# Feed-forward input chunks as seven block products over half the tokens, with d_ff in two groups

## What is computed

```python
x = x + 0.5 * swiglu_ffn(rms_norm(x, ffn1_norm), ffn1_w_in, ffn1_w_out)
h = rms_norm(x, mix_norm)
q, k, v, xr, gate = split(h @ w_in_proj)        # differential attention | RG-LRU branch
x = x + concat([y_attn, y_rnn]) @ w_out_proj
x = x + 0.5 * swiglu_ffn(rms_norm(x, ffn2_norm), ffn2_w_in, ffn2_w_out)

def swiglu_ffn(h, w_in, w_out):
    g, u = split(h @ w_in, 2)
    return (silu(g) * u) @ w_out
```

## Time and profile before

| | before |
|---|---|
| median of 3 runs | 938.46 us (938.35 to 939.8) |
| time of the profiled execution | 938.35 us |
| its span, first to last instruction | 936.5 us |
| TensorE busy | 922.3 us, 98% |
| VectorE busy | 482.4 us, 52% |
| ScalarE busy | 331.1 us, 35% |
| DMA engines, mean | 27% |

### The profile page before, as it was taken

The page is one execution under the profiler, slowest core; times in us unless marked ns, Lnnn a source line. Parts: engine busy times, 40 slices in busy tenths (PEclk is TensorE's granted clock), DMA queues, the critical chain, the costliest instruction groups (busy, mean ns, idle before and its releaser), DMA issues.

```text
span 936.5 us, 11101 instructions
## 1 busy us (share of the span) xinstructions
PE 922.3 (98%) x4154; PEld 754.2 (81%) x4154; DVE 482.4 (52%) x712; ACT 331.1 (35%) x526; POOL 3.1 (0%) x25
## 2 busy tenths in 40 slices
PE   8999999999999999999997999999999999999998
PEld 7888888888888888777885678888888888888887
DVE  6754444444444346665879776645444444422221
ACT  7422222332223233356647654332222233211220
POOL 0000000000000000000000000000000000000000
PEclk9999999999999999999999999999999999999999
DMA  7222222222222224222221022322233222132241
GB/s 272 97 90 95 113 106 90 90 90 76 90 95 92 92 95 154 97 83 90 91 90 45 1 91 70 111 90 90 90 105 119 90 90 76 63 122 92 92 140 42
DMA packets 16295, 89.13 MB, mean 95 GB/s; under 512 B 2064, under 2 KB 2192, under 8 KB 8976
## 3 DMA queue, kind: packets, MB, share of 16 engines
q1 hardware_dynamic: 16128, 88.32, 27.1%
q0 software_dynamic: 144, 0.52, 0.2%
HBM read 86.74 MB, written 2.10 MB: 95 GB/s over the span
## 4 chain that ended last, share of the span: by engine, by line
PE 95%; DVE 2%; ACT 1%; DMA 1%; issue 1%; SPq 0%; ACTq 0%
PE bank L975 31%; PE bank L977 30%; PE bank L976 30%; PE bank L1172 1%; PE bank L1115 1%; PE bank L1149 1%; DMA raw<-w_in_dram 1%; PE bank L1162 0%; PE bank L1089 0%; DVE h_lo L599 0%; DVE small L896 0%; ACT w_hi L341 0%; PE bank L990 0%; ACT sq L518 0%; DVE yr_lo L803 0%
## 5 line engine op out<-in xcount | busy, mean ns | idle before, releaser
L975 PE MATMUL bank<-h_hi,w_hi 128*128 128x512 f32 x768 | 301.4, 392 | 0.9 <-DVE w_lo L587 0.8
L977 PE MATMUL bank<-h_hi,w_lo 128*128 128x512 f32 x768 | 298.9, 389 | 0.0
L976 PE MATMUL bank<-h_lo,w_hi 128*128 128x512 f32 x768 | 298.9, 389 | 0.0
L587 DVE TENSOR_TENSOR w_lo<-raw,w_hi 128x1024 fp32r<-128x1024 f32 (+1 forms) x178 | 188.7, 1101 | 79.5 <-ACT w_hi L341 73.9
L341 ACT ACTIVATE w_hi<-raw 128x1024 fp32r<-128x1024 f32 (+1 forms) x178 | 160.9, 951 | 159.9 <-PE bank L977 159.9
L975 PEld LDWEIGHTS bank<-h_hi,w_hi 128*128 128x128 f32 x768 | 144.1, 188 | 32.9 <-DVE w_lo L587 1.2
L976 PEld LDWEIGHTS bank<-h_lo,w_hi 128*128 128x128 f32 x768 | 144.2, 188 | 30.9 <-issue 1.2
L977 PEld LDWEIGHTS bank<-h_hi,w_lo 128*128 128x128 f32 x768 | 144.2, 188 | 30.1
L975 PE MATMUL bank<-act_hi,w_hi 128*128 128x512 f32 x352 | 136.9, 389 | 0.0
L976 PE MATMUL bank<-act_lo,w_hi 128*128 128x512 f32 x352 | 136.9, 389 | 0.0
L977 PE MATMUL bank<-act_hi,w_lo 128*128 128x512 f32 x352 | 136.9, 389 | 0.0
(11 more groups left out here) (173 smaller groups left out, 656.7 us busy)
## 6 DMA issues: line engine op xcount, KB each, us to landing
raw<-w_in_dram SPq DMA_DIRECT2D x43, 1024.0 KB, 4.8
raw<-w_out_dram SPq DMA_DIRECT2D x32, 704.0 KB, 4.0
raw<-w_qkv_dram SPq DMA_DIRECT2D x6, 1024.0 KB, 4.8
raw<-w_rnn_dram SPq DMA_DIRECT2D x4, 1024.0 KB, 4.7
raw<-w_proj_dram SPq DMA_DIRECT2D x4, 1024.0 KB, 4.8
x<-xT_dram SPq DMA_DIRECT2D x8, 256.0 KB, 6.0
out_dram<-x SPq DMA_DIRECT2D x8, 256.0 KB, 5.0
raw<-w_in_dram SPq DMA_DIRECT2D x4, 256.0 KB, 6.0
```

What stands on the lines that cost most here:

```text
L587: dve.tensor_tensor(w_lo[:, part], raw[:, part], w_hi[:, part].bitcast(F32), ALU.subtract).then_inc(low_made, 1)
L975: pe.matmul(dst, s_hi, m_hi, start=first, stop=False)
L976: pe.matmul(dst, s_hi, m_lo, start=False, stop=False)
L977: return pe.matmul(dst, s_lo, m_hi, start=False, stop=last)
```

## The change

Of the 22 input chunks of each feed-forward, the first 4 (ffn1) or 2 (ffn2) stay as they were ("P", plain). The others ("W") compute gate and up for all 512 tokens by Strassen's scheme in its form by Winograd: the weights of a pair of k-tiles are a 2 x 2 of 128x128 blocks (k parity by gate or up), the two k-tiles of h another 2 x 2 of 128x256 blocks (k parity by earlier or later 256 tokens). In place of eight block products there are seven, `seven_products`, each over 4 pairs and three parts, 84 products of 256 columns. Ops 1, 4 and 6 take weight blocks as they are, ops 0, 2, 3 and 5 take sums of them; ops 0, 2, 3 and 6 take sums of blocks of h (T1 to T4). Ops 3 to 6 add onto what ops 0 to 2 left in three half banks, after it has been read.

- GpSimd makes T1 to T4 once for each feed-forward (`blocks_of_h`), ScalarE and VectorE their highs and lows (`t_highs`, `t_lows`).
- VectorE makes the four weight sums (`s123`, `s4`) and their lows (`s_lows`); ScalarE their highs (`s_highs`).
- The lows of the three plain blocks: ScalarE writes the negated highs (`minus_highs`), and an SBUF to SBUF transfer from GpSimd's queue adds the raw weights onto them (`a_lows`).
- ScalarE copies two partial results (`copies`); VectorE combines the seven into gate and up (`take_q6` to `up_later`).

d_ff is worked in groups of 10 and 12 tiles: 10 input chunks, 8 output chunks of 10 k-tiles, 12 input chunks, 8 output chunks of 12. Each output tile is therefore taken out of PSUM twice. Half rstd multiplies there, no longer in up. The programs of SP, ScalarE and VectorE are unrolled in the feed-forwards; TensorE keeps its loops. The sine and exponential of ScalarE stand under the first group's output chunks. The core of the diff (added lines; what is left out are counts, layout, and the same helpers without their slot argument):

```diff
+GROUP = (10, 12)
+FIRST_TILE = (0, GROUP[0])
+PLAIN = (4, 2)
...
+        t_hi = region("t_hi", [P, 2 * KT * SEQ], F32R, tile_at(36))
+        t_lo = region("t_lo", [P, 2 * KT * SEQ], F32R, tile_at(52))
...
+        B12, B11, B22, B21, T1, T2, T3, T4 = range(8)
+        MOVING = (T2, B11, T1, T3, B21, B22, T4)
+        def s_place(op, s):
+            at = {1: s * SLOT, 4: s * SLOT + BLOCK, 6: s * SLOT + 2 * BLOCK, 0: A_COLS, 5: SLOT + A_COLS, 2: 0, 3: BLOCK}[op]
+            return (ws_hi, ws_lo, at) if op in (2, 3) else (w_hi, w_lo, at)
+        def s_parts(op):
+            hi, lo, at = s_place(op, 0)
+            return hi[:, at:at + BLOCK], lo[:, at:at + BLOCK]
+        S_OPS = (0, 2, 3, 5)
...
+        def part_bank(c, n):
+            return bank[3 * (c % 2) + n][:, 0:HALF]
...
+        T_STEPS = (((), (0,), (1, 2), (3,)), ((0, 1), (2, 3)))
...
+            def consumed(c):
+                if kind(c) == "W":
+                    w = wino_of(c)
+                    sp.wait_ge(high_made, 2 * c + 2)
+                    sp.wait_ge(s13_made, 2 * w + 2)
+                    sp.wait_ge(s4_made, w + 1)
+                    sp.wait_ge(low_landed[c % 2], 16 * (w // 2 + 1))
+                else:
+                    sp.wait_ge(low_made, lows_through(c))
...
+            def blocks_of_h(f):
+                gain_col = (COL_G1, COL_G2)[f]
+                pool.wait_ge(h_low, 2 * KT * f + KT)
+                for p in range(KT // 2):
+                    buf = pairbuf[p % 2]
+                    b = lambda n: buf[:, n * HALF:(n + 1) * HALF]
+                    if p >= 2:
+                        pool.wait_ge(t_low, KT // 2 * f + p - 1)
+                    for r in range(2):
+                        k = 2 * p + r
+                        step(pool.tensor_scalar(buf[:, r * SEQ:(r + 1) * SEQ], tile(x, k), cols[:, gain_col + k:gain_col + k + 1],
+                                                None, ALU.mult))
+                    step(pool.tensor_tensor(b(T1), b(B11), b(B12), ALU.subtract))
+                    step(pool.tensor_tensor(b(T2), b(B22), b(T1), ALU.add))
+                    step(pool.tensor_tensor(b(T3), b(B12), b(B22), ALU.subtract))
+                    step(pool.tensor_tensor(b(T4), b(B21), b(T2), ALU.subtract))
+                    pool.sem_inc(t_sums, 1)
+            def a_lows(c):
+                w = wino_of(c)
+                pool.wait_ge(minus_made, w + 1)
+                at = c % 2 * SLOT
+                pool.dma_start(w_lo[:, at:at + A_COLS].bitcast(F32), raw[:, at:at + A_COLS],
+                               accum_op=ALU.add).then_inc(low_landed[c % 2], 16)
...
+            def minus_highs(c):
+                at = c % 2 * SLOT
+                act.wait_ge(raw_landed[c % 2], 16 * (c // 2 + 1))
+                act.wait_ge(chunk_used, c + 1)
+                act.activation(w_lo[:, at:at + A_COLS], raw[:, at:at + A_COLS], ACT.Copy, scale=-1.0).then_inc(minus_made, 1)
+            def a_highs(c):
+                at = c % 2 * SLOT
+                for j in range(2):
+                    part = slice(at + j * A_COLS // 2, at + (j + 1) * A_COLS // 2)
+                    act.activation(w_hi[:, part], raw[:, part], ACT.Copy).then_inc(high_made, 1)
+            def s_highs(c, op, last_user=None):
+                w = wino_of(c)
+                act.wait_ge(*{2: (s13_made, 2 * w + 1), 0: (s2_made, w + 1), 3: (s13_made, 2 * w + 2), 5: (s4_made, w + 1)}[op])
+                if last_user is not None:
+                    act.wait_ge(chunk_used, USED(last_user))
+                elif w:
+                    act.wait_ge(op_done, 6 * w - 6 + op + 1)
+                hi, _, at = s_place(op, 0)
+                act.activation(hi[:, at:at + BLOCK], s_sum(op), ACT.Copy).then_inc(s_high, 1)
+            def copies(c, n):
+                w = wino_of(c)
+                act.wait_ge(op_done, 6 * w + n + 1)
+                act.activation((q6_copy, q1_copy)[n](c), part_bank(c, 1 - n), ACT.Copy).then_inc(copied, 1)
+            def silu(f, c):
+                t = FT * f + tile_of(c - C_FFN[f])
+                act.wait_ge(g_scaled, t + 1)
+                act.activation(both(gate_s, c), both(gate_s, c), ACT.Silu).then_inc(silu_made, 1)
+            def act_highs(f, c):
+                n = tile_of(c - C_FFN[f])
+                act.wait_ge(prod_made, FT * f + n + 1)
+                act.activation(tile(act_hi, n - FIRST_TILE[n >= GROUP[0]]), both(up_s, c), ACT.Copy).then_inc(act_high, 1)
...
+            def plain_step(f, c):
+                following = kind(c + 1)
+                k = c - C_FFN[f]
+                if following == "P" and k >= 2:
+                    highs(c + 1, IN_COLS)
+                if following == "W":
+                    minus_highs(c + 1)
+                    s_highs(c + 1, 0, c - 1)
+                    a_highs(c + 1)
+                    s_highs(c + 1, 2)
+                    s_highs(c + 1, 3)
+                for p in T_STEPS[f][k]:
+                    t_highs(f, p)
+                silu(f, c)
+                if following == "W":
+                    s_highs(c + 1, 5, c)
+                act_highs(f, c)
+            def wino_step(f, c):
+                following = kind(c + 1)
+                if following == "W":
+                    minus_highs(c + 1)
+                else:
+                    highs(c + 1, OUT_COLS[c - C_FFN[f] >= IN_AT[1]])
+                if kind(c - 1) == "W":
+                    act_highs(f, c - 1)
+                copies(c, 0)
+                if following == "W":
+                    s_highs(c + 1, 0)
+                copies(c, 1)
+                if following == "W":
+                    a_highs(c + 1)
+                    for op in S_OPS[1:]:
+                        s_highs(c + 1, op)
+                silu(f, c)
+                if following == "O":
+                    act_highs(f, c)
...
+            def s123(c):
+                w = wino_of(c)
+                dve.wait_ge(raw_landed[c % 2], 16 * (c // 2 + 1))
+                if w:
+                    dve.wait_ge(s_low, 4 * w - 1)
+                dve.tensor_tensor(s_sum(2), raw_block(c, 3), raw_block(c, 2), ALU.add).then_inc(s13_made, 1)
+                dve.tensor_tensor(s_sum(3), raw_block(c, 0), raw_block(c, 3), ALU.add).then_inc(s13_made, 1)
+                dve.wait_ge(s13_made, 2 * w + 1)
+                if w:
+                    dve.wait_ge(s4_made, w)
+                    dve.wait_ge(s_low, 4 * w - 3)
+                dve.tensor_tensor(s_sum(0), s_sum(2), raw_block(c, 0), ALU.add).then_inc(s2_made, 1)
+            def s4(c):
+                w = wino_of(c)
+                dve.wait_ge(s2_made, w + 1)
+                if w:
+                    dve.wait_ge(s_low, 4 * w)
+                dve.tensor_tensor(s_sum(5), s_sum(0), raw_block(c, 1), ALU.add).then_inc(s4_made, 1)
+            def s_lows(c, op):
+                dve.wait_ge(s_high, 4 * wino_of(c) + S_OPS.index(op) + 1)
+                hi, lo = s_parts(op)
+                dve.tensor_tensor(lo, s_sum(op), hi.bitcast(F32), ALU.subtract).then_inc(s_low, 1)
...
+            def take_q6(c):
+                w = wino_of(c)
+                dve.wait_ge(copied, 2 * w + 2)
+                if w >= 2:
+                    dve.wait_ge(post, 5 * w - 6)
+                dve.tensor_tensor(q16(c), q1_copy(c), q6_copy(c), ALU.subtract).then_inc(t_made, 1)
...
+            def take_q5(c):
+                w = wino_of(c)
+                dve.wait_ge(op_done, 6 * w + 3)
+                if w >= 2:
+                    dve.wait_ge(post, 5 * w - 8)
+                dve.tensor_tensor(q15(c), part_bank(c, 2), q1_copy(c), ALU.add).then_inc(post, 1)
...
+            def up_earlier(c):
+                w = wino_of(c)
+                dve.wait_ge(post, 5 * w + 1)
+                dve.wait_ge(act_low, count_of(c) - 1)
+                dve.wait_ge(op_done, 6 * w + 4)
+                dve.tensor_tensor(half(up_s, c, 0), part_bank(c, 1), q15(c), ALU.subtract).then_inc(post, 1)
+            def gate_later(c):
+                w = wino_of(c)
+                dve.wait_ge(op_done, 6 * w + 5)
+                dve.wait_ge(prod_made, count_of(c) - 1)
+                dve.tensor_tensor(half(gate_s, c, 1), part_bank(c, 0), rstd[:, LATER], ALU.mult).then_inc(post, 1)
+            def gate_earlier(c):
+                w = wino_of(c)
+                dve.wait_ge(t_made, w + 1)
+                dve.wait_ge(op_done, 6 * w + 6)
+                dve.tensor_tensor(half(gate_s, c, 0), part_bank(c, 2), q16(c), ALU.add).then_inc(post, 1)
+                dve.wait_ge(post, 5 * w + 4)
+                dve.tensor_tensor(half(gate_s, c, 0), half(gate_s, c, 0), rstd[:, EARLIER], ALU.mult).then_inc(g_scaled, 1)
+            def up_later(c):
+                dve.wait_ge(chunk_used, USED(c))
+                dve.tensor_tensor(half(up_s, c, 1), part_bank(c, 1), q1_copy(c), ALU.subtract).then_inc(post, 1)
...
+            def plain_step(f, c):
+                k = c - C_FFN[f]
```

(119 more changed lines are left out.)

547 lines of the change are left out of this document (315 added, 232 removed).

## The result

The changed kernel takes 951.99 us (951.12 to 952.31) where the kernel before takes 938.4: a ratio of 1.014, 95% interval 1.0122 to 1.0157. It is 13.6 us slower, and the forecast was 1.0 us faster. Its profiled execution has a span of 950.1 us, against 936.5.

What follows compares the result with a forecast made beforehand. TensorE's product count bounds the old kernel, the ScalarE-VectorE ring the changed block chunks: 38 chunks fall from 413.4 to 411.1 us, plus 1.3 for end and table, so 938.4 - 1.0 = 937.4; own range 925 to 948, overall 912 to 960.

Steps and rivals of the forecast that it cites:

- the price of GpSimd's block sums: Block sums of h on GpSimd: 2.1 to 6.3 us a pair, 4 taken, with 0 to 4 us lost.
- First chunk with its wait: First block chunk of each feed-forward, waiting for sums and the Q6 copy: 22.2 us in ffn2, 12.6 in ffn1.
- The first chunks of the long groups: First block chunk of each 12-chunk group, its sums made under the last output chunk: some 9.8 us each.
- The other 34 block chunks: The remaining block chunks, each set by the ring at 10.49 us, 34 x 10.49 in the sum.
- the ring: Ordered waits between ScalarE and VectorE from one block chunk's `gate_earlier` to the next: 10.49 us a chunk.
- one gap a chunk: TensorE stands about 0.9 us in every block chunk, at op 3, waiting for ScalarE's Q6 copy.
- the accumulating transfer: SBUF to SBUF transfer of 768 KB in each block chunk: 6.1 us taken, costing nothing up to about 10.
- the rival that decides from 11 us: Accumulating transfer is slow and sets the block chunk; at 12 us the kernel takes 956; chance 0.18.
- Weight loads hide under the short products: TensorE's loads overlap 256-column products; the rival, that they don't, gives some 1234 us, chance 0.03.
- rival of 0.13 us a product: 256-column products on TensorE take 0.13 us, a block chunk 10.92, the kernel 952 us; chance 0.05.
- The first rival: TensorE stays the bound because a ring link is not one: 904 us, or 923 at 0.120 a product; chance 0.10.

Runs made afterwards that it cites:

- The last experiment: VectorE's gate first in the last plain step, added to the kernel with four plain chunks, split block sums and later A highs (926.45 us): 922.45 us, ratio 0.983.
- Reordering: ScalarE makes the highs of sums 2 and 3 ahead of the A highs, against the changed kernel (951.99 us): 942.97 us, ratio 1.0048.

## Why the prediction was wrong

**The step that failed** is the price of GpSimd's block sums. The prediction bounded a pair by the earlier trace rows, a memset of 512 columns at 0.52 us, from below at 2.1 us and from above at three times the memset, 6.3, and took 4. Measured are 1.6 us for a 512-column multiplication and 0.73 for 256 columns at the least, and 6.9 to 8.0 us for a pair in ffn2, 7.5 to 9.1 in ffn1. Even the upper bound was under the true cost. A memset has no input, and a factor on it was a guess. Nor are memsets all that GpSimd does in the kernel before, as the prediction has it: one operation there reads a tile (groups by form, busy us, mean ns).

```profile
L309 POOL TENSOR_SCALAR_AFFINE_SELECT ident<-ident 128x128 f32<-128x128 f32 x1 | 0.3, 284 | 0.2 <-POOL ident L307 0.2
...
L301 POOL MEMSET ones<- 128x128 f32 x1 | 0.2, 203 | 0.0
```

It takes 1.4 times the memset of its size. A 512-column multiplication at that rate would be 0.73 us, an estimate, and still less than half of the 1.6: this row would have warned of a higher price, but not given it.

The prediction left up to 5.4 us for each pair free and named 0 to 4 us as lost, of which its sum has nothing. It became 8.5 us lost in ffn2 and 4.6 in ffn1 (5.8 us between the starts against 1.2 without the sums); with 1.3 us of the next point that is 14.4 of the 14.6 that leaving them out gave back. The kernel without them measured the forecast, 937.42 for 937.4.

In ffn1 GpSimd also stood idle ahead of its third pair:

```profile
37.41 1.57 POOL L467 TENSOR_SCALAR pairbuf<-x,cols 128x512 f32<-128x512 f32 x1 [4.50 <-DVE t_lo L870]
```

There are two pair buffers, and the third pair waits until VectorE has made the T lows of the first, which stand in its second step. The last sum was ready at 54.25. At the forecast's 4 us a pair it would have been ready at 45.4 even with this wait, 8.8 us earlier (an estimate from these rows), and the 4.6 us would not have been lost. Without the wait, at GpSimd's measured price, it would have come 4.3 us earlier; a third buffer was not tried.

The Trainium skill (GPSIMD Engine Reference, 4.1 Engine selection) puts GpSimd at some 2 times slower than VectorE for elementwise operations with two inputs, and at about line rate with one. For two inputs the trace agrees (0.73 against 0.42 us, 1.7 times); for the multiplication by a column, one tensor input, it does not: 1.6 against 0.5 us. By these two statements of the Trainium skill and VectorE's durations a pair would have been some 4.4 us, an estimate near what I took.

**Second, the price that GpSimd puts on VectorE,** which the sum did not have at all. VectorE's sum of squares in ffn1 (timeline, changed kernel, then the one without block sums):

```profile
20.23 5.78 DVE L850 TENSOR_TENSOR sq_sum<-sq_sum,sq 128x512 f32<-128x512 f32 x5
```

```profile
19.30 3.87 DVE L843 TENSOR_TENSOR sq_sum<-sq_sum,sq 128x512 f32<-128x512 f32 x5
```

Five operations in 5.78 us instead of 3.87; `s123`'s first two take 1.2 us each beside GpSimd and 0.68 without. GpSimd's own 256-column sums take 0.73 or, in turns with VectorE, 1.07 to 1.60. TensorE's sum of squares came 2.2 us later than before and waited 1.3 us. The Trainium skill (SBUF — State Buffer, Who interferes with whom) says that a VectorE instruction with two SBUF inputs contends with a GpSimd instruction that reads SBUF. The trace agrees, with these numbers.

**The terms beside it.** First chunk with its wait: 31.5 us in ffn2 for 22.2, 19.2 in ffn1 for 12.6, together 15.9 over. Without the block sums they are 22.9 and 14.6, so in ffn2 the order was read rightly and in ffn1 2 us were missing by themselves: op 3 there waits 3.3 us for the Q6 copy, because ScalarE's silu of the plain chunk waits for a gate that VectorE makes only after the sums for two chunks. The last experiment takes that away. The first chunks of the long groups: 10.07 for 9.8. The other 34 block chunks: 352.5 us for 356.7, 4.2 under. With the 1.3 us at the sum of squares that is 13.5 of the 14.6 us; about 1 us is not placed. The forecast's match with the kernel without block sums rests partly on such small errors of both signs.

**Right:** the ring. 10.39 us for 10.49, link by link: from silu to VectorE's `s_lows` (2) 245.50 to 251.10, 5.60 us, and 0.46 ahead of it make 6.06 for 6.18; the VectorE part is 4.33 for 4.31. VectorE at 83% and ScalarE at 63% for the 80 and 65 forecast; one gap a chunk, ahead of op 3, from ScalarE's copy. It was 0.3 us where 0.9 was foreseen, because a 256-column product takes 0.120 us, not 0.1133: the 0.0133 us beyond the columns stays whole. The prediction had named that value and that nothing hangs on it below 0.125, which held. With the ring gone it is the floor, 10.08.

**Right:** the accumulating transfer, 5.7 us for 6.1, without a gap before op 1 in the steady chunks (in the kernels with four plain chunks and with split sums TensorE waited for it once, 0.7 and 0.8 us, in ffn2's second group); the rival that decides from 11 us did not come near. Weight loads hide under the short products: 0.120 us holds both, and all products use all rows, so the rule of the Trainium skill that the prediction cited (TensorE: Matmul & The Clock Gate, Part 3, The mechanism) and doubted does not hold here. The same section also lets a load go ahead when it targets the background weight buffer; that would fit, but no run here shows which buffer a load takes. The prediction's rival of 0.13 us a product came to 952, the time that was measured, but by another cause: the products take 0.120 us.

**The first rival** (TensorE stays the bound, 923 at 0.120) did not occur, since each link held. Reordering made it occur: 9 us in 38 chunks.

## What to carry to other kernels

An engine that has hardly more than memsets in the trace has no known price for arithmetic; a factor on a memset is no bound, and what waits for the first result of such an engine has to be costed at several times it. Where a scheme replaces one engine's products by side work on three others, look for the ring of waits between these: its length, not their busy time, is what the bound engine sees, and program order on one of them can be worth more than the work. Put the work on the ring first and the rest where the engine idles: here that, with more cover for the start and half of the sums on VectorE, turned 1.4% slower into 1.7% faster.

## What was not expected of the hardware

- GpSimd: 1.6 us for a multiplication of 512 columns by a column of gains, 0.73 us for a sum of 256; VectorE has 0.50 and 0.42 for the same.
- VectorE's 512-column additions of two SBUF tiles take 1.2 us instead of 0.68 while GpSimd computes from SBUF.
- After the long wait in ffn2 TensorE's granted clock was 0.50, its 1.2 GHz level, for some 3.4 us, to 619.5 us; it had fallen during the wait:

```profile
610.00:616.30 6.30, 0.13 (x1) 0.50 0.32 62
616.30:618.90 2.60, 2.60 (x12) 0.50 0.76 151
618.90:629.70 10.80, 9.39 (x74) 0.97 0.65 171
```

(Stretches of the changed kernel, TensorE alone: length, busy us with count, clock, DMA, GB/s.) Products start 0.213 us apart there, 256 columns at 1.2 GHz and nothing beyond, so that the 0.0133 us shows only at the higher level. In the changed kernel it cost nothing: with the sums left out, ffn1's first block chunk had op 0 at full clock and took the same 13.4 us, since op 3 waits for ScalarE in either. In the last version, where op 3 no longer waits, the slow op 0 shows: 11.7 us in ffn1, 10.2 in ffn2, where the clock stood at its full level.
